# Moving the adaLN product of a two-layer hybrid trunk in among the weight stages, and handing norm sums, mixed blocks and the store over block by block

## The chip, the cores and the metric

The kernel runs on one core of a Trainium2 chip. The metric is the time on the device in microseconds (us), the median of several runs. TensorE is called PE, VectorE DVE, ScalarE ACT, GpSimd POOL and SyncE SP, as in the profile.

## The reference, cut to what matters

Sequence of 512 tokens, model width 1024, float32 throughout, two layers with weights of their own.

```python
c_act = silu(c)                                   # one row of 1024
for l in range(2):
    ada = c_act @ w_ada[l] + b_ada[l]             # 1024 x 6144, a matrix-vector product
    sh1, sc1, g1, sh2, sc2, g2 = split(ada, 6)
    h = rms_norm(x, norm1_g[l]) * (1 + sc1) + sh1
    z, xbc, dt, q, k, v, gate_s, gate_a = split(h @ w_in[l])
    y_ssm = mamba2(z, conv4(xbc), dt) @ w_ssm_out[l]
    y_att = diff_attention(q, k, v) @ w_attn_out[l]
    mixed = sigmoid(gate_s) * y_ssm + sigmoid(gate_a) * y_att
    x = x + g1 * (mixed @ w_out[l])
    h = rms_norm(x, norm2_g[l]) * (1 + sc2) + sh2
    x = x + g2 * (square(relu(h @ w_ff1[l])) @ w_ff2[l])
return rms_norm(x, final_g)
```

Norm 1 needs sh1 and sc1 only; g1 is needed after attention, sh2 and sc2 at norm 2, g2 in the second half of the feed-forward.

## The kernel before

Activations lie transposed, as 8 blocks k of 128 channels by 512 tokens. A weight matrix is streamed as units of 1024 x 256 (1 MB). There are 88 of them in a layer, in this order: 4 for B and C (bc) and 8 for the conv input (xs), together the conv stages; 8 gates; 16 of z and ssm_out; 12 of q, k and v; 4 attn_out (AO); 4 out (WO); 32 of the feed-forward (ff), which run as 4 rounds of 4 units of w_ff1 and 4 of w_ff2. Units alternate between two slots. Three pipelined steps stand ahead of PE's use of a unit:

- SP loads it into `raw[slot]`, once POOL has finished the unit two before (`lo_ready`, L311 and `units`).
- ACT rounds it to `w_hi[slot]` (`convert`, L732). It waits for the load, and for PE to be done with the unit two before (`gemm_done`).
- POOL forms the rest `w_lo[slot]` in four instructions (`low`, L1485).

PE then does 48 matmuls, three products (hi*hi, hi*lo, lo*hi) for each of 8 blocks k and 2 halves j of the unit (`unit_rows`, L384 to L386); k is the outer loop, so both output banks are complete at the end of the unit together. ACT and DVE empty the banks. **Every engine's program is one fixed list**, written out by hand; engines meet only through semaphores. In the lists that matter here, unit n+2 is converted on ACT ahead of the evacuation of unit n:

- Conv stages: ACT converts unit n+2, then seeds the two conv blocks of unit n (L791); DVE adds three taps to each (L1187), ACT takes tanh (L797), DVE makes silu of both (L1197).
- Feed-forward, first half of a round: ACT converts unit n+2, then does relu and square of unit n (L1025, L1027), DVE the low part (L1455, L1458), all of which the second half multiplies (`squared`, at its first unit). Second half: DVE alone adds to x (L1464).

The **adaLN product** has 24 pieces of 1 MB per layer. It stands at the start of each layer, ahead of norm 1 and of all units. Twelve pieces go through DVE: a multiply and seven multiply-adds of 256 columns (L1130, L1134), then PE sums the partitions in 4 instructions (L454). Twelve go through PE (L448), in `raw`, and back through ACT (L772) and 48 small matmuls (L462). Then comes norm 1 (L1090, L749, L1095), block by block, and the product for dt (L471); a long chain of small DVE operations on dt stands ahead of the first taps.

At a norm, ACT squares the 8 blocks of x (L744), DVE sums them (L1071, L1073), PE sums over partitions (L424), DVE takes the mean (L1078), POOL the rsqrt (L1478), PE spreads it (L430). All of this begins when the last block of x is complete. `mixed` is handed from DVE to ACT in the same way after the last block, and `out` is stored by one DMA after the last block of y_out.

The loops over layers, the bc and xs rounds and the ff rounds are hardware loops (`Fori`).

## Time and profile before

| | us |
|---|---|
| median of 3 runs (lowest, highest) | 2994.64 (2994.18, 3003.76) |
| the profiled execution, its own time | 3004.83 |
| its span, first to last instruction | 3003.0 |
| PE / DVE / ACT / POOL busy in the span | 2574.0 / 1322.4 / 960.4 / 1086.1 |
| raw and ada loads | 224 of 1 MB |
| mean granted clock of TensorE | 0.914 |

Times in rows are us from the start of the span. A row of the timeline gives start, length, engine, line, operation, tiles, count, and in brackets how long the engine had been idle and what ended that. Rows of merged instructions (xN) run from the first to the end of the last. Matmuls are pipelined, so that PE's busy time says little; the distance from one to the next, or from one unit to the next, is what to read.

### The profile page before, as it was taken

To read this page: it belongs to the slowest core of one execution; us is meant where nothing else is said; L and a number is where in the kernel's file an instruction comes from. 1 tells how busy PE (TensorE), PEld (TensorE's weight loads), DVE (VectorE), ACT (ScalarE), POOL (GpSimd) and SP (SyncE) were. 2 spreads that over 40 slices of the span, in tenths; PEclk is the share of its full clock that TensorE was granted. 3 is DMA by queue.
4 is the path that set the end of the run, shared out by engine and by line. 5 is a ranking of instruction groups with operands and counts; after the bars stand their busy time and mean duration, and the time that the engine had idled before them with its cause. 6 is when DMAs were issued, how large, how long until landed. Compare 5 with 4: busy or idle time off the path is not lost.

```text
span 3003.0 us, 36626 instructions
## 1 busy us (share of the span) xinstructions
PE 2574.0 (86%) x12200; PEld 2051.4 (68%) x12200; DVE 1322.4 (44%) x2019; ACT 960.4 (32%) x1532; POOL 1086.1 (36%) x825
## 2 busy tenths in 40 slices
PE   5798889788888697999977988988898877799997
PEld 2586667687666476888735866676776655688885
DVE  5654434332655326333366444433335552343333
ACT  1244332322544223222212443332334442232221
POOL 0244343334322144555402443433343222445552
PEclk9899989899989698999978999998999977899998
DMA  7421111122111121222273211011121111212221
GB/s 300 175 84 70 42 42 42 66 75 77 59 55 43 43 91 64 98 98 98 97 302 116 84 57 52 32 57 70 70 91 56 43 43 57 84 71 98 98 98 56
DMA packets 34516, 251.56 MB, mean 84 GB/s; under 512 B 3824, under 2 KB 4208, under 8 KB 4976
## 3 DMA queue, kind: packets, MB, share of 16 engines
q1 hardware_dynamic: 34416, 250.30, 22.8%
q8 instruction: 54, 0.88, 0.1%
q14 instruction: 46, 0.38, 0.0%
HBM read 244.00 MB, written 6.29 MB: 83 GB/s over the span
## 4 chain that ended last, share of the span: by engine, by line
issue 51%; POOL 23%; PE 11%; POOLq 9%; DVE 3%; DMA 2%; ACT 1%; DVEq 0%; PEld 0%; PEldq 0%; ACTq 0%; SPq 0%
POOL w_lo L1485 21%; POOLq L1487 7%; PE gemm L384 3%; PE gemm L385 2%; PE gemm L386 2%; PE aux L448 2%; DMA raw<-stream 2%; POOL y_tok L1526 1%; POOL smalls L1478 1%; DVE conv L1187 1%; POOL xdt L1517 1%; POOLq L1522 1%; PE aux L416 0%; POOLq L1518 0%; DVE pre L1090 0%
## 5 line engine op out<-in xcount | busy, mean ns | idle before, releaser
L1485 POOL TENSOR_TENSOR w_lo<-raw,w_hi 128x512 fp32r<-128x512 f32 x704 | 963.9, 1399 | 1590.0 <-ACT w_hi L732 1588.6
L384 PE MATMUL gemm<-h_hi,w_hi 128*128 128x512 f32 x1536 | 647.3, 421 | 37.9 <-POOLq L1487 10.1
L732 ACT ACTIVATE w_hi<-raw 128x2048 fp32r<-128x2048 f32 x176 | 336.6, 1914 | 939.9 <-PE gemm L386 849.3
L385 PE MATMUL gemm<-h_lo,w_hi 128*128 128x512 f32 x1536 | 614.1, 400 | 0.0
L386 PE MATMUL gemm<-h_hi,w_lo 128*128 128x512 f32 x1536 | 613.3, 399 | 0.0
L384 PEld LDWEIGHTS gemm<-h_hi,w_hi 128*128 128x128 f32 x1536 | 298.5, 194 | 135.5 <-issue 59.9
L384 PE MATMUL gemm<-op_hi,w_hi 128*128 128x512 f32 x896 | 362.4, 404 | 26.6 <-POOLq L1487 23.0
L385 PE MATMUL gemm<-op_lo,w_hi 128*128 128x512 f32 x896 | 359.5, 401 | 0.0
L386 PE MATMUL gemm<-op_hi,w_lo 128*128 128x512 f32 x896 | 358.3, 400 | 0.0
L385 PEld LDWEIGHTS gemm<-h_lo,w_hi 128*128 128x128 f32 x1536 | 298.8, 195 | 69.6 <-issue 12.0
L386 PEld LDWEIGHTS gemm<-h_hi,w_lo 128*128 128x128 f32 x1536 | 297.6, 194 | 65.4
L402 PE MATMUL gemm<-w_hi,h_hi 128*128 128x256 f32 x768 | 233.1, 304 | 1.6 <-issue 1.6
L403 PE MATMUL gemm<-w_hi,h_lo 128*128 128x256 f32 x768 | 227.6, 296 | 0.0
L404 PE MATMUL gemm<-w_lo,h_hi 128*128 128x256 f32 x768 | 227.1, 296 | 0.0
L384 PEld LDWEIGHTS gemm<-op_hi,w_hi 128*128 128x128 f32 x896 | 175.1, 195 | 67.5 <-issue 16.2
L386 PEld LDWEIGHTS gemm<-op_hi,w_lo 128*128 128x128 f32 x896 | 174.9, 195 | 37.9
L385 PEld LDWEIGHTS gemm<-op_lo,w_hi 128*128 128x128 f32 x896 | 175.2, 196 | 36.5
L1455 DVE TENSOR_TENSOR usq<-relu 128x512 f32<-128x512 f32 x64 | 93.0, 1453 | 196.7 <-ACTq L1026 191.4
L402 PEld LDWEIGHTS gemm<-w_hi,h_hi 128*128 128x128 f32 x768 | 158.9, 207 | 10.2 <-issue 9.8
L1187 DVE SCALAR_TENSOR_TENSOR conv<-gemm,cw,conv 128x511 f32<-128x511 f32 x144 | 107.8, 749 | 122.6 <-ACT conv L791 98.0
L403 PEld LDWEIGHTS gemm<-w_hi,h_lo 128*128 128x128 f32 x768 | 159.0, 207 | 0.4
L404 PEld LDWEIGHTS gemm<-w_lo,h_hi 128*128 128x128 f32 x768 | 157.9, 206 | 0.0
(171 smaller groups left out, 2861.3 us busy)
## 6 DMA issues: line engine op xcount, KB each, us to landing
raw<-stream SPq DMA_DIRECT2D x200, 1024.0 KB, 4.8
ada_raw<-stream SPq DMA_DIRECT2D x24, 1024.0 KB, 7.2
xsave<-x SPq DMA_DIRECT2D x2, 2048.0 KB, 12.6
x<-xsave SPq DMA_DIRECT2D x2, 2048.0 KB, 7.8
x<-xT SPq DMA_DIRECT2D x1, 2048.0 KB, 7.7
out<-y_out SPq DMA_DIRECT2D x1, 2048.0 KB, 6.3
dtw_raw<-dtw SPq DMA_DIRECT2D x2, 512.0 KB, 8.0
rope_cos<-ropes SPq DMA_DIRECT2D x2, 256.0 KB, 2.7
```

The lines of the kernel that those rows point to most:

```text
L384: mm(o, w_hi[:, slot, k, cols], hi[:, k, :], start=k == 0, stop=False)
L385: mm(o, w_hi[:, slot, k, cols], lo[:, k, :], start=False, stop=False)
L386: last = mm(o, w_lo[:, slot, k, cols], hi[:, k, :], start=False, stop=k == KB - 1)
L402: mm(o, h_hi[:, k, toks], w_hi[:, slot, k, :], start=k == 0, stop=False)
L403: mm(o, h_lo[:, k, toks], w_hi[:, slot, k, :], start=False, stop=False)
L404: last = mm(o, h_hi[:, k, toks], w_lo[:, slot, k, :], start=False, stop=k == KB - 1)
L448: last = mm(ab[2 + s][0:1, 0:UW], cact[:, k:k + 1], raw[:, s, k, :], start=k == 0, stop=k == KB - 1)
L732: A(w_hi[:, slot], raw[:, slot], ACT.Copy).then_inc(hi_ready, 1)
L1187: last = STT(conv[:, c, lag:S], gb[c][:, 0:S - lag], cw[:, bass.ds(block * CONV + (CONV - 1 - lag), 1)], conv[:, c, lag:S], ALU.mult, ALU.add)
L1455: TT(usq[:, j], relu[:, c], relu[:, c], ALU.mult)
L1485: gp.tensor_tensor(w_lo[:, slot, ks], raw[:, slot, ks], w_hi[:, slot, ks].bitcast(F32), ALU.subtract)
L1487: pool.drain().then_inc(lo_ready, 1)
```

## The change

The adaLN product is spread out. **FIRST**: 8 pieces of layer 0 (sh1, sc1), all loaded at the start into 8 places of their own; 4 go through PE directly, with the piece as the stationary operand (16 float32 matmuls), 4 through DVE. **EARLY**: 12 pieces of layer 0 in its 12 conv units, one behind each unit's silu on DVE. **LATE**: 28 pieces (4 of layer 0, all 24 of layer 1) in the feed-forward of layer 0, one behind each unit's work on DVE. Early and late pieces have two buffers each, and go through DVE only. Their loads are issued by SP between the loads of the units; PE sums each over the partitions behind the next unit. Layer 1 computes nothing of it at its start.

Squares and sums of the norms, `mixed` with its high and low parts, and the store of `out` go block by block. In units whose operands are ready, PE does half j = 0 before j = 1. The bc, xs and ff loops on SP, PE and DVE and the layer loops are written out. x is saved to `xsave` in layer 1 only.

```diff
-ADA_H, ADA_Q, UNITS_H = ADA // 2, ADA // 4, UNITS // 2
+FIRST = [(0, m) for m in (4, 0, 5, 1, 6, 2, 7, 3)]
+EARLY = [(0, m) for m in range(8, 20)]
+LATE = [(0, m) for m in range(20, 24)] + [(1, m) for m in range(ADA)]
+N_FIRST, N_EARLY, N_LATE = len(FIRST) // 2, len(EARLY), len(LATE)
+LATE_ROUND = 8
...
         def sp_program(sp):
+            def unit(l, n):
+                if l * UNITS + n >= 2:
+                    sp.wait_ge(lo_ready, l * UNITS + n - 1 + LO_CREDIT)
+                load(l, n)
...
+            for n in range(N_FIRST):
+                piece(ada_pe[n], *FIRST[2 * n], pe_in[n])
+                piece(ada_first[n], *FIRST[2 * n + 1], first_in[n])
+                if n == 0:
+                    sp.dma_start(x[:], xT).then_inc(x_in, 16)
+                    load_par(0)
+                    load_dtw(0)
+            for l in range(DEPTH):
+                for n in range(U_GATE):
+                    unit(l, n)
+                    if l and n == 1:
+                        sp.wait_ge(S_["layer"], l + LAYER_CREDIT)
+                        sp.dma_start(xsave, x[:]).then_inc(x_saved, 16)
+                    if l == 0:
+                        if n == 0:
+                            sp.wait_ge(ada_step, step_at(N_FIRST - 1))
+                        elif n == 1:
+                            sp.wait_ge(aux_full[2], total_at(l, "start", "bank2", 0) + 1)
+                        else:
+                            sp.wait_ge(ada_step, step_at(N_FIRST + n - 2))
+                        piece(ada_early[n % 2], *EARLY[n], early_in[n % 2])
...
+                for n in range(U_FF, UNITS):
+                    unit(l, n)
+                    i, u = divmod(n - U_FF, 8)
...
+                    m = i * LATE_ROUND + u
+                    if l == 0 and m < N_LATE:
+                        if m == 0:
+                            sp.wait_ge(S_["mixed"], total_at(l, "mix", "mixed", KB))
+                        if m >= 2:
+                            sp.wait_ge(ada_step, step_at(N_FIRST + N_EARLY + m - 2))
+                        piece(ada_late[m % 2], *LATE[m], late_in[m % 2])
...
+            for k in range(KB):
+                sp.wait_ge(S_["pre"], DEPTH * TOTAL["pre"] + k + 1)
+                sp.dma_start(out[:, k], y_out[:, k]).then_inc(out_done, 16)
...
         def pe_program(pe):
+            def ada_piece(where, bank, c):
+                for j in range(2):
+                    for k in range(KB):
+                        last = mm(bank[:, c + j:c + j + 1], where[:, k, j * P:(j + 1) * P], cact[:, k:k + 1], ...)
+            def ada_column(n, acc, bank, c):
+                pe.wait_ge(ada_step, step_at(n))
+                for j in range(2):
+                    last = mm(bank[:, c + j:c + j + 1], acc[:, n % 2, j * P:(j + 1) * P], ones[:, 0:1], start=True, stop=True)
+                last.then_inc(ada_out, 1)
...
+                if l:
+                    norm_spread(st)
+                if l == 0:
+                    for n in range(N_FIRST):
+                        pe.wait_ge(pe_in[n], 16)
+                        ada_piece(ada_pe[n], ab[3], 2 * FIRST[2 * n][1])
+                        ada_column(n, ada_acc, ab[3], 2 * FIRST[2 * n + 1][1])
+                    pe.drain().then_inc(ada_full, 1)
+                    norm_spread(st)
...
+                for i in range(4):
                     sf = Step(l, "ff", i)
                     for u in range(4):
...
+                        if l == 0 and i * LATE_ROUND + u:
+                            late(i * LATE_ROUND + u - 1)
                     for u in range(4):
...
+                        if l == 0 and i * LATE_ROUND + u + 3 < N_LATE:
+                            late(i * LATE_ROUND + u + 3)
...
         def act_program(act):
                 for u in range(N_WO):
-                    convert(l, U_WO // 2 + 1 + u // 2, u % 2)
-                act.wait_ge(S_["x_sum"], st("x_sum") + 1)
-                squares_of_x(st)
+                    if u < N_WO - 1:
+                        convert(l, U_WO // 2 + 1 + u // 2, u % 2)
+                    squares_of_x(st, range(2 * u, 2 * u + 2))
+                convert(l, U_WO // 2 + 1 + (N_WO - 1) // 2, (N_WO - 1) % 2)
...
         def dve_program(dve):
+                def early(n):
+                    if l == 0:
+                        ada_piece(N_FIRST + n, ada_early[n % 2], (early_in[n % 2], (n // 2 + 1) * 16), ada_acc)
                 def conv_round(step, base, block, dst):
                     for c in range(4):
                         taps(step, base, c // 2, c % 2, block + c)
                         if c % 2:
                             silu(step, c - 1, dst(c - 1))
                             silu(step, c, dst(c))
+                            early(2 * base + c // 2)
...
+                for i in range(4):
                     for u in range(4):
                         for j in range(2):
...
+                        late(i * LATE_ROUND + u)
                     for u in range(4):
                         for j in range(2):
...
+                        if i < 3:
+                            late(i * LATE_ROUND + 4 + u)
```

The waits in front of `convert` on ACT, and its place ahead of the seeds and the relus, are the same in both kernels. On POOL the program of the last norm is the same; at norm 2 the rsqrt stands behind `low` of the first two ff units, as before.

## Rows read from the trace of the kernel before

**Rows 1.** Timeline of a ff round, layer 0: ACT, DVE, then POOL.
```profile
1246.20 1.92 ACT L732 ACTIVATE w_hi<-raw 128x2048 fp32r<-128x2048 f32 x1 [8.96 <-PE gemm L386]
...
1248.67 1.37 DVE L1455 TENSOR_TENSOR usq<-relu 128x512 f32<-128x512 f32 x1 [12.59 <-ACTq L1026]
...
1253.51 1.62 DVE L1458 TENSOR_TENSOR op_lo<-usq,op_hi 128x512 fp32r<-128x512 f32 x1
...
1248.20 6.39 POOL L1485 TENSOR_TENSOR w_lo<-raw,w_hi 128x512 fp32r<-128x512 f32 x4 [5.85 <-ACT w_hi L732]
...
1302.60 5.03 POOL L1485 TENSOR_TENSOR w_lo<-raw,w_hi 128x512 fp32r<-128x512 f32 x4 [5.85 <-ACT w_hi L732]
```

**Rows 2.** Timeline of DVE, one adaLN piece; below it, of PE, its sum.
```profile
27.70 0.35 DVE L1130 TENSOR_SCALAR ada_acc<-ada_raw,first 128x256 f32<-128x256 f32 x1 [1.01 <-issue]
...
28.09 3.61 DVE L1134 SCALAR_TENSOR_TENSOR ada_acc<-ada_raw,first,ada_acc 128x256 f32<-128x256 f32 x7
...
35.16 0.61 PE L454 MATMUL aux<-first,ada_acc 128*128 128x1 f32 x4
```

**Rows 3.** DMA issues of the page: count, KB each, median us to landing.
```profile
raw<-stream SPq DMA_DIRECT2D x200, 1024.0 KB, 4.8
ada_raw<-stream SPq DMA_DIRECT2D x24, 1024.0 KB, 7.2
...
out<-y_out SPq DMA_DIRECT2D x1, 2048.0 KB, 6.3
```

**Rows 4.** Timeline of the conv stages, layer 0: ACT, then DVE.
```profile
175.40 1.92 ACT L732 ACTIVATE w_hi<-raw 128x2048 fp32r<-128x2048 f32 x1 [1.75 <-PE gemm L386]
...
256.44 1.92 ACT L732 ACTIVATE w_hi<-raw 128x2048 fp32r<-128x2048 f32 x1 [1.82 <-PE gemm L386]
...
150.97 1.30 DVE L1197 SCALAR_TENSOR_TENSOR bct<-ctanh,conv 128x512 f32 x2 [0.25 <-issue]
...
183.92 1.30 DVE L1197 SCALAR_TENSOR_TENSOR bct<-ctanh,conv 128x512 f32 x2 [0.25 <-issue]
```

**Rows 5.** Timeline, start of layer 0: first squares, the sum over partitions, norm 1.
```profile
16.69 1.13 ACT L744 ACTIVATE sq<-x 128x512 f32<-128x512 f32 x2
...
24.62 1.86 PE L424 MATMUL aux<-first,ss 128*128 128x1 f32 x8 [24.62 <-DVEq L1076]
...
103.67 1.41 DVE L1090 SCALAR_TENSOR_TENSOR pre<-x,amul,aux 128x512 f32<-128x512 f32 x2 [0.18 <-issue]
```

**Rows 6.** Timeline of DVE, end of layer 0 to the first taps of layer 1.
```profile
1495.77 1.43 DVE L1464 SCALAR_TENSOR_TENSOR x<-gemm,ada,x 128x512 f32<-128x512 f32 x2 [9.45 <-PE gemm L386]
...
1591.16 1.41 DVE L1090 SCALAR_TENSOR_TENSOR pre<-x,amul,aux 128x512 f32<-128x512 f32 x2 [0.18 <-issue]
...
1632.24 0.75 DVE L1187 SCALAR_TENSOR_TENSOR conv<-gemm,cw,conv 128x511 f32<-128x511 f32 x1 [0.53 <-issue]
```

**Rows 7.** Timeline, end of attn_out to the first ff unit, layer 0: ACT, DVE.
```profile
1077.50 1.91 ACT L732 ACTIVATE w_hi<-raw 128x2048 fp32r<-128x2048 f32 x1 [8.96 <-PE gemm L386]
...
1094.26 1.92 ACT L732 ACTIVATE w_hi<-raw 128x2048 fp32r<-128x2048 f32 x1 [9.97 <-PE gemm L386]
...
1159.16 1.92 ACT L732 ACTIVATE w_hi<-raw 128x2048 fp32r<-128x2048 f32 x1 [3.51 <-PE gemm L386]
...
1126.23 1.43 DVE L1443 SCALAR_TENSOR_TENSOR x<-gemm,first,x 128x512 f32<-128x512 f32 x2 [9.45 <-PE gemm L386]
...
1144.24 1.41 DVE L1090 SCALAR_TENSOR_TENSOR pre<-x,amul,aux 128x512 f32<-128x512 f32 x2 [3.37 <-PE aux L430]
```

**Rows 8.** Timeline of DVE, the last norm.
```profile
2977.14 1.43 DVE L1464 SCALAR_TENSOR_TENSOR x<-gemm,ada,x 128x512 f32<-128x512 f32 x2 [9.45 <-PE gemm L386]
...
2980.05 5.39 DVE L1073 TENSOR_TENSOR ss<-ss,sq 128x512 f32<-128x512 f32 x7
...
2990.96 5.36 DVE L1090 SCALAR_TENSOR_TENSOR y_out<-x,con,aux 128x512 f32<-128x512 f32 x8 [3.30 <-PE aux L430]
```

**Rows 9.** The page's granted clock of TensorE in 40 slices, tenths of full speed.
```profile
PEclk9899989899989698999978999998999977899998
```

More of the change, by code:

```diff
@@ L1064, in dve_program, with norm_add @@
             dve.drain().then_inc(ready, 1)
-            def norm_sums(step):
-                for k in range(KB):
+            def norm_add(step, ks):
+                for k in ks:
                     dve.wait_ge(S_["sq"], step("sq") + 1)
@@ L1079, in norm_sums, with ada_piece, take_ada, scales @@
                 dve.drain().then_inc(S_["ms"], 1)
+            def ada_piece(n, where, landed, acc):
+                dve.wait_ge(*landed)
+                for k in range(KB):
+                    if k == 0:
+                        dve.wait_ge(ada_out, n - 1 + OUT_CREDIT)
+                        TS(acc[:, n % 2], where[:, 0], cact[:, 0:1], None, ALU.mult).then_inc(ada_step, 1)
+                    else:
+                        dve.wait_ge(ada_step, n * KB + k)
+                        STT(acc[:, n % 2], where[:, k], cact[:, k:k + 1], acc[:, n % 2], ALU.mult, ALU.add)\
+                            .then_inc(ada_step, 1)
+            def take_ada(nth, l, bank, c, first, last):
+                dve.wait_ge(ada_full, nth)
+                cols = slice(first * KB, last * KB)
+                dve.wait_ge(par_in, (l + 1) * 16)
+                TT(ada[:, cols], bank[:, c:c + (last - first) * KB],
+                   par[:, C_BADA + first * KB:C_BADA + last * KB], ALU.add)
+                dve.drain().then_inc(ada_read, 1)
+            def scales(m):
+                scale_at, norm_at = ((1, C_N1), (4, C_N2))[m]
+                STT(amul[:, m * KB:(m + 1) * KB], ada_v[:, scale_at, :], 1.0,
+                    par[:, norm_at:norm_at + KB], ALU.add, ALU.mult)
+                settle()
             def norm(step, mul, shift):
@@ L1489, in pool_program @@
             pool.sem_inc(lo_ready, LO_CREDIT)
-            pool.sem_inc(ada_out, 2)
             pool.wait_ge(ready, 1)
-            with pool.Fori(0, DEPTH) as l:
+            for l in range(DEPTH):
                 st = Step(l, "start")
+                if l:
+                    low(l, 0, 0)
                 rsqrt(ms, rs, st, "ms", "rs")
-                low(l, 0, 0)
+                if l == 0:
+                    low(l, 0, 0)
                 low(l, 0, 1)
```

380 lines of the change are left out of this document (214 added, 166 removed).

## The prediction

> **What bounds the kernel now.** I read the timeline first, one stage at a time, because the page calls PE 86% busy and that hides which stages run at PE's own pace. In a feed-forward round [rows 1] POOL starts the low part of one unit at 1248.20 and that of the fifth after it at 1302.60: 10.88 us per unit, with nothing between units. That is PE's pace at full clock, and ACT, DVE and POOL have slack: ACT starts converting unit n+2 when unit n is done (1246.20, I call this moment C), POOL is done with it at C + 8.4 (C + 7.2 where it takes 5.03), and PE wants it at C + 10.9. The conv stages run close to this (C from 175.40 to 256.44, [rows 4]). What stands outside that pace is the start of a layer: the adaLN product keeps norm 1 waiting until 103.67 in layer 0 [rows 5], and from 1496.4, where the last unit ends, to 1591.16 in layer 1 [rows 6]. Then come norm 2, the step from attn_out to out, and the tail.
>
> So the change removes real path. The question is what 40 pieces cost where they go, and the timeline of those stages holds the answer too: the order inside [rows 1] is convert of n+2 first, then relu, squares and low part of unit n, ended on DVE at 1255.13 (1253.51 + 1.62), which is C + 8.9. In the conv stages it is convert of n+2, then seeds, taps, tanh and silu of unit n, ended at C + 9.8 (175.40 to 185.22, [rows 4]).
>
> **What the change gains.**
>
> *Norm 1, layer 0.* x now lands behind two pieces, with 4.4 MB queued up to it in place of the 2.3 MB, and ACT squares it first. In the old order squares begin at 16.69 behind the parameters and dt's weights, and the sums end at 24.6 [rows 5]; I put them at about 21.5. The first piece began 3.1 behind the sums (27.70, [rows 2]); dt's low part and the parameter work now come in between, some 2 more; then four pieces of 4.0 (0.35 + 3.61 and one start): 42.6. PE does its 4 pieces, 16 matmuls each, which are 32 instructions (its 2 column sums are 4 in [rows 2]). At the 0.15 us of its column sums (0.61 for 4, [rows 2]) one takes 4.9, at the 0.23 of the cold sums (1.86 for 8, [rows 5]) 7.4. With a column sum behind each that ends at 23.5 + 22 = 45.5, or 55.5. Norm 1 then begins at 45.5 to 58. PE warms up while it works, so I take 46: a gain of 58 us (46 to 60).
>
> *Layer 1's start.* After the last unit at 1496.4: one add to x (0.75, half of 1495.77's row), square and sum of the last block (1.7, from half of 1.13 in [rows 5] and a seventh of 5.39 in [rows 8], with two hand-overs), the take of the last sixth of ada (0.5), then mean, rsqrt and spread, 5.5 us by the last norm (sums end 2985.44, y_out begins 2990.96, [rows 8]). Norm 1 begins 8.9 after the end of the unit, at 1505.3 in place of 1591.16. Behind it stands dt's chain up to the first taps at 1632.24, unchanged but for a convert of 1.9 on ACT that now stands ahead of norm 1: 86 + 1, so **87 us** (85 to 90).
>
> *Out units.* From convert to convert 1077.50 to 1094.26 is 16.8 [rows 7] where PE's pace gives 10.9. With 2 blocks left to hand over instead of 8 PE starts at once; ACT's convert then comes a little behind the last two: 5 us per layer, 10 (8 to 12).
>
> *Norm 2.* Squares, sums and mean end 9.8 us earlier, but POOL's rsqrt stands behind the low part of the second ff unit, whose convert ACT now does after the last squares: convert from D + 1.5, low part until D + 8.7 (5.03 and waits), rsqrt 1.0, spread 2.1, with D the end of the out units, 1126.1. Norm 2 begins at D + 12.1, not at D + 18.1 (1144.24, [rows 7]): 6 us per layer, 12 (10 to 20).
>
> *The tail.* Sums end at D + 2.5 in place of 2985.44 with D = 2977.1 [rows 8], 5.9 earlier; the store of 2 MB takes 6.3 to land [rows 3], the last eighth perhaps 2.7: 9.5 (6 to 10).
>
> Gains: 58 + 87 + 10 + 12 + 9.5 = **177 us**. Half order j by itself I cost at nothing: convert stands ahead of every evacuation and waits for both halves. So do the written-out loops: at the round boundaries inside the rows above PE's pace has no gap. Between -5 and +10.
>
> **What it costs.** SP's list now reads: load unit n; wait for piece n-2; load piece n; load unit n+1. Piece n-2 stands on DVE behind the silu (or the low part) of unit n-2, and these stand on ACT behind the convert of unit n. **That is a loop**: convert n, evacuation of n-2, piece n-2, loads of piece n and unit n+1, convert n+1. Before, the load of n+1 waited for POOL alone, with a unit's time to spare. `raw` has two places, but the wait in SP's list takes the second away.
>
> Its length: 9.8 + 4.0 (piece) + 0.2 + landing. A load alone lands in 4.8, one with others in flight in 7.2 [rows 3]. The unit's load goes 0.3 behind the piece, through the same engines: I take 7.2 from the piece's issue, with 5.1 and 8.5 as the ends. In the conv stages 21.2 per unit, in the first half of an ff round 8.9 + 4.0 + 0.2 + 7.2 = 20.3, against 10.9.
>
> *Conv stages, layer 0.* In the old times: silu of unit 0 ends at 152.3 (150.97 + 1.30, [rows 4]), piece 0 at 156.3, unit 3 lands at 163.7; nine turns of 21.2 bring the convert of unit 12 to 354.5, where it was 256.44. The tail adds little: piece 10 at 368, taps and silu of unit 11 (7), piece 11 (4), sum and take (1) end at 380.6; before, about 279.5 (convert of unit 13 at 268, 9.8, and 1.5 of transposes). **+101 us**. The PE column sums (12 of 0.6, [rows 2]) vanish in PE's idle time.
>
> *Feed-forward, layer 0.* Count from the convert C that starts when unit 0 of a round is done. Four turns bring the convert of unit 6 to C + 81.2. From there PE is the bound: unit 6 may start at + 8.4, and it, 7 and 8 take 10.9 + 2 x 11.4 (with a column sum each) up to + 42.1. In the second half a piece follows the adds to x directly, so its loads (issued 5.2 after the unit's end, landed 12.6) are in time. A round takes 123.3 in place of 87.0: 3 x 36.3 = 109. In the last round pieces stop after the fourth: one turn (20.3), then 78 to its end, 98.4 for 76.2: 22. Together 131.
>
> Here a row speaks for more. In the second half a piece (two operands in SBUF) runs beside POOL's low part. In [rows 1] POOL's four instructions take 6.39 beside DVE's squares, 5.03 alone, and DVE's own take 1.37 to 1.62 there. Pieces of 6.5 instead of 4.0, and 8 for POOL, push the second halves past PE's pace by about 2.5 us each and more at the change of halves: +10 (0 to 20). The Trainium skill (SBUF — State Buffer, on the port pair that VectorE and GpSimd share) says that a VectorE instruction with two SBUF inputs and a GpSimd one that reads SBUF exclude each other for their whole length. By that the pieces would be nearer the upper end, +16. The rows agree that both get slower. Feed-forward: **+141 us**.
>
> **The sum.** 101 + 141 - 177 = **+65 us**. It is made against the profiled execution (3004.83, of which 3003.0 is span), which lies 10.2 above the median of the runs shown. I carry the difference over to the median: 2994.6 + 65 = **3060 us**, 2.2% slower. The turns of the two loops enter some 23 times, so 1 us in a turn is 23 us in the result.
>
> **Rivals.**
>
> *The pieces ride free.* DVE is 44% busy, the DMA engines mostly idle, and if each load were in raw by the time its convert can start, only the column sums (about 20 us) and 6 us at the end of the conv stages would be left: 177 - 26 gained, **2844**. It takes a turn of no more than 10.9 + the 2.5 to 3.7 of slack that ACT and POOL leave. Against it: the landing alone is 4.8, the evacuation 8.9. It decides only if the order convert, evacuation, piece, load is not what binds, for example if pieces were done by DVE before the evacuation. 0.12.
>
> *The clock falls.* PE would now idle some 9 us in every 20 in the bound halves. The granted clock falls with gaps in PE's work: it is 6 tenths from 975 to 1050, where attention runs out, 7 and 8 from 1500 to 1650, around the adaLN product of layer 1, and 9 in the dense stages [rows 9]; of its two levels, 1.2 and 2.4 GHz, that is the lower for part of the time. In a turn a unit at half speed (twice 10.9) still fits, as PE is not the bound there; but at each change to the second half and at the conv stages' end a slow unit adds up to 10: 3 x 10 + 10, **3100**. The Trainium skill (TensorE: Matmul & The Clock Gate, on oscillation of the gate) warns of just such a rhythm of work and waits. 0.10.
>
> *Lighter loops.* The second load lands close to the first's time, 5.1, and PE's pieces are quick: 2.1 x 23 = 48 less, **3012**, or about no change with every gain at its upper end. 0.08.
>
> *The first part does not help.* The eight pieces ahead of norm 1 are as late as the old product because eleven MB stand in one queue. But the second of two loads lands 2.4 behind the first (7.2 less 4.8, [rows 3]), so eleven are in by about 31, ahead of the last piece: unlikely; +20 at worst, **3080**, inside the range.
>
> **How the numbers follow.** Forecast 0.67, free pieces 0.12, clock 0.10, lighter loops 0.08, rest 0.03. The range of **3000 to 3110** takes in the cases of the clock and of the lighter loops, and the bounds of the landing (-48, +30) and of the port (-10, +10) laid on the forecast; it leaves out the free pieces alone. What a measurement can tell from no change is about 0.3%, 9 us: faster 0.13, same 0.04, slower 0.83.
>
> **What would show it.** In the profile after: on layer 0's conv stages converts 21 us apart, with SP's wait for DVE's pieces (not POOL) ahead of each load, and ACT's convert waiting for the DMA; in layer 0's feed-forward four slow units and four at PE's pace; layer 1's same stages at their old pace; norm 1 of layer 0 near 46, that of layer 1 some 9 us behind the last unit, norm 2 12 us behind; POOL's rsqrt there behind its low part. I am wrong if layer 0's converts stay 11 to 12 us apart, or if the wait before them is for PE.

## The result and the profile after

The changed kernel takes **3052.17 us** (median of 4 runs, 3052.11 to 3055.09), the kernel before 2994.85 in the same comparison: a ratio of 1.0187, 95% interval 1.0167 to 1.0207. The profiled execution took 3052.11 us, 3050.3 of it span. The forecast was 3060 with a range of 3000 to 3110, slower with 0.83.

First the page, the lines that answer to [rows 3, 9] and the convert's own line:

```profile
span 3050.3 us, 33323 instructions
...
PE 2541.0 (83%) x11928; PEld 2068.2 (68%) x11928; DVE 1440.2 (47%) x2182; ACT 949.4 (31%) x1508; POOL 1101.7 (36%) x825
...
PEclk9888899998999698889898999989989996999999
...
L820 ACT ACTIVATE w_hi<-raw 128x2048 fp32r<-128x2048 f32 x176 | 336.7, 1914 | 1134.1 <-DMA raw<-stream 448.1
...
raw<-stream SPq DMA_DIRECT2D x176, 1024.0 KB, 4.8
```

Read the convert's line (L820), ACT's rounding of a unit: of its 1134 us of idle time 448 now end with the arrival of a load (35 waits) and 685 with PE. In the kernel before it was one wait of 9 us for a load and 929 us for PE. Yet half of the loads still land in 4.8 us or less. The transfers aren't slow, they are issued late. Why is in the waits of SP's queue:

```profile
engine line waited for: us in total, times, longest us
SPq L327 <- POOLq L1651: 2049.0, 133, 45.0
SPq L323 <- DVE late_acc L1200: 427.3, 26, 42.3
SPq L323 <- DVE ada_acc L1200: 240.1, 11, 32.2
```

Of the 176 loads of units only 133 still wait for POOL. 37 pieces wait for DVE, 667 us in all, and unit loads stand behind them. One turn in the conv stages, unit by unit the answer to [rows 4] (ACT, DVE, then SP):

```profile
196.13 1.92 ACT L820 ACTIVATE w_hi<-raw 128x2048 fp32r<-128x2048 f32 x1 [12.05 <-DMA raw<-stream]
...
216.41 1.92 ACT L820 ACTIVATE w_hi<-raw 128x2048 fp32r<-128x2048 f32 x1 [10.08 <-DMA raw<-stream]
...
203.82 1.29 DVE L1325 SCALAR_TENSOR_TENSOR xsf<-ctanh,conv 128x512 f32<-128x512 f32 x2
...
205.41 3.61 DVE L1200 SCALAR_TENSOR_TENSOR ada_acc<-ada_early,first,ada_acc 128x256 f32<-128x256 f32 x7
...
209.05 0.33 SPq L323 DMA_DIRECT2D ada_early<-stream  x1
209.42 0.43 SPq L327 DMA_DIRECT2D raw<-stream  x1
```

The convert starts at 196.13, the silus end 9.0 later, the piece 3.9 after that, SP issues at once (209.05, and the unit's load at 209.42), and the next convert starts at 216.41: a turn of 20.3 us. The same in the feed-forward, where a piece of the second half looks different (DVE, then POOL; compare [rows 1, 2]):

```profile
1205.90 3.61 DVE L1200 SCALAR_TENSOR_TENSOR late_acc<-ada_late,first,late_acc 128x256 f32<-128x256 f32 x7
...
1267.75 7.33 DVE L1200 SCALAR_TENSOR_TENSOR late_acc<-ada_late,first,late_acc 128x256 f32<-128x256 f32 x7
...
1268.69 5.58 POOL L1649 TENSOR_TENSOR w_lo<-raw,w_hi 128x512 fp32r<-128x512 f32 x4 [2.68 <-ACT w_hi L820]
```

And the norms (timeline: PE's first piece and its column sum, DVE at norm 1 of layer 0, at norm 2, at layer 1's start, at the end; they answer to [rows 5 to 8]):

```profile
22.19 6.97 PE L458 MATMUL aux<-first,ada_pe 128*128 128x1 f32 x32
29.01 0.99 PE L466 MATMUL aux<-first,ada_acc 128*128 128x1 f32 x4
...
53.13 0.17 DVE L1208 TENSOR_TENSOR ada<-aux,par 128x16 f32<-128x16 f32 x1 [11.33 <-PEq L518]
...
55.39 1.41 DVE L1228 SCALAR_TENSOR_TENSOR pre<-x,amul,aux 128x512 f32<-128x512 f32 x2 [1.79 <-PE aux L504]
...
1149.22 0.75 DVE L1581 SCALAR_TENSOR_TENSOR x<-gemm,g1h,x 128x512 f32<-128x512 f32 x1 [4.43 <-PE gemm L441]
...
1160.82 1.40 DVE L1228 SCALAR_TENSOR_TENSOR pre<-x,amul,aux 128x512 f32<-128x512 f32 x2 [7.83 <-PE aux L504]
...
1666.28 0.75 DVE L1620 SCALAR_TENSOR_TENSOR x<-gemm,ada,x 128x512 f32<-128x512 f32 x1 [1.52 <-PE gemm L441]
...
1673.84 1.41 DVE L1228 SCALAR_TENSOR_TENSOR pre<-x,amul,aux 128x512 f32<-128x512 f32 x2 [3.30 <-PE aux L504]
...
3042.28 5.36 DVE L1228 SCALAR_TENSOR_TENSOR y_out<-x,con,aux 128x512 f32<-128x512 f32 x8 [3.27 <-PE aux L504]
```

To see where the time went I laid the starts of ACT's converts side by side (176 in each trace, 88 per layer). Each figure is the length of a stretch in us:

| stretch, from convert to convert | before, layer 0 / 1 | after, layer 0 / 1 |
|---|---|---|
| start to unit 2 (layer 1: from unit 87 of layer 0) | 134.9 / 148.1 | 86.7 / 54.6 |
| conv stages, 2 to 12 | 121.6 / 121.5 | 211.2 / 123.8 |
| 12 to 20 (end of conv, scan) | 213.1 / 206.4 | 208.7 / 206.1 |
| 20 to 50 (z, attention) | 575.4 / 575.6 | 566.5 / 565.7 |
| 50 to 58 (attn_out, out, norm 2) | 114.3 / 114.3 | 102.8 / 103.1 |
| feed-forward, 58 to 87 | 315.5 / 315.5 | 468.7 / 315.6 |
| unit 87 of layer 1 to the end | 46.9 | 36.9 |

Two stretches lose (the ones in which layer 0 carries pieces: 90 and 153 us), layer 1's same stretches stay. And one line nobody had on the bill: z and attention are 8.8 and 9.9 us shorter, though no edit touches them.

### The profile page after: what moved, and what is told of

It reads as the page before. It is cut to its first block, busy times and chain, and to the rows that moved or that the text cites. A ratio compares the mean times of both kernels' runs of the same rounds, so it can differ in the third digit from the quotient of the medians.

```text
span 3050.3 us, 33323 instructions
## 1 busy us (share of the span) xinstructions
PE 2541.0 (83%) x11928; PEld 2068.2 (68%) x11928; DVE 1440.2 (47%) x2182; ACT 949.4 (31%) x1508; POOL 1101.7 (36%) x825
## 4 chain that ended last, share of the span: by engine, by line
issue 39%; POOL 19%; PE 14%; DVE 10%; POOLq 7%; ACT 4%; DMA 3%; DVEq 2%; ACTq 1%; SPq 0%; PEldq 0%; PEld 0%
POOL w_lo L1649 17%; POOLq L1651 6%; DMA raw<-stream 2%; DVE conv L1315 2%; PE gemm L428 2%; PE gemm L430 2%; PE gemm L429 2%; DVE ada_acc L1200 1%; PE gemm L439 1%; PE gemm L441 1%; PE gemm L440 1%; ACT probs L1052 1%; PE aux L458 1%; PE aux L488 1%; POOL y_tok L1694 1%
## 5 line engine op out<-in xcount | busy, mean ns | idle before, releaser
L1649 POOL TENSOR_TENSOR w_lo<-raw,w_hi 128x512 fp32r<-128x512 f32 x704 | 978.1, 1419 | 1673.3 <-ACT w_hi L820 1672.2
L820 ACT ACTIVATE w_hi<-raw 128x2048 fp32r<-128x2048 f32 x176 | 336.7, 1914 | 1134.1 <-DMA raw<-stream 448.1
L439 PE MATMUL gemm<-h_hi,w_hi 128*128 128x512 f32 x960 | 394.7, 411 | 12.0 <-DVE conv L1315 7.0
L440 PE MATMUL gemm<-h_lo,w_hi 128*128 128x512 f32 x960 | 388.8, 405 | 0.0
L441 PE MATMUL gemm<-h_hi,w_lo 128*128 128x512 f32 x960 | 387.4, 404 | 0.0
L428 PE MATMUL gemm<-h_hi,w_hi 128*128 128x512 f32 x576 | 263.6, 458 | 10.2 <-DVE h_lo L1233 4.9
L430 PE MATMUL gemm<-h_hi,w_lo 128*128 128x512 f32 x576 | 234.0, 406 | 0.0
L429 PE MATMUL gemm<-h_lo,w_hi 128*128 128x512 f32 x576 | 233.7, 406 | 0.0
L439 PEld LDWEIGHTS gemm<-h_hi,w_hi 128*128 128x128 f32 x960 | 191.2, 199 | 53.0 <-issue 7.4
L441 PEld LDWEIGHTS gemm<-h_hi,w_lo 128*128 128x128 f32 x960 | 189.5, 197 | 42.0
L440 PEld LDWEIGHTS gemm<-h_lo,w_hi 128*128 128x128 f32 x960 | 190.5, 198 | 39.7
L1601 DVE TENSOR_TENSOR usq<-relu 128x512 f32<-128x512 f32 x64 | 93.5, 1462 | 244.9 <-ACTq L1133 241.9
L440 PE MATMUL gemm<-op_lo,w_hi 128*128 128x512 f32 x512 | 203.0, 396 | 0.0
L441 PE MATMUL gemm<-op_hi,w_lo 128*128 128x512 f32 x512 | 203.0, 396 | 0.0
```

The lines of the kernel that those rows point to most:

```text
L428: mm(o, w_hi[:, slot, k, cols], hi[:, k, :], start=k == 0, stop=False)
L429: mm(o, w_hi[:, slot, k, cols], lo[:, k, :], start=False, stop=False)
L430: last = mm(o, w_lo[:, slot, k, cols], hi[:, k, :], start=False, stop=k == KB - 1)
L439: mm(o, w_hi[:, slot, k, cols], hi[:, k, :], start=k == 0, stop=False)
L440: mm(o, w_hi[:, slot, k, cols], lo[:, k, :], start=False, stop=False)
L441: last = mm(o, w_lo[:, slot, k, cols], hi[:, k, :], start=False, stop=k == KB - 1)
```

## Experiments

All ratios are against the kernel before, run on the same chip in the same comparison (median 2998.92 us for conv_order, both_order, both_lag and warm, 3001.25 for before_written_out, rows_order, rsqrt_first and warm18, 2999.88 for piece_first, split, all_three and all_split).

| kernel | us | ratio, 95% interval |
|---|---|---|
| conv_order | 2983.23 | 0.9959 (0.9938 to 0.9979) |
| both_order | 2866.05 | 0.9557 (0.9534 to 0.9579) |
| both_lag | 2840.14 | 0.9474 (0.9457 to 0.9492) |
| piece_first | 2836.81 | 0.9466 (0.9429 to 0.9503) |
| warm | 3053.27 | 1.0184 (1.0165 to 1.0204) |
| warm18 | 3057.64 | 1.0182 (1.0165 to 1.0199) |
| before_written_out | 2978.95 | 0.9926 (0.9912 to 0.9940) |
| rows_order | 3058.97 | 1.0185 (1.0169 to 1.0201) |
| rsqrt_first | 2830.74 | 0.9434 (0.9421 to 0.9447) |
| split | 2831.77 | 0.9439 (0.9423 to 0.9455) |
| all_three | 2866.10 | 0.9550 (0.9534 to 0.9565) |
| all_split | 2870.36 | 0.9568 (0.9553 to 0.9583) |

### The loop, cut at SP

`upto(l, n)` issues the loads of units, each with its wait for POOL as before, up to unit n.

```diff
 for n in range(U_GATE):
-    unit(l, n)
+    upto(l, n + 2)          # conv_order, both_order
     ...
     piece(ada_early[n % 2], *EARLY[n], early_in[n % 2])
 for n in range(U_FF, UNITS):
-    unit(l, n)
+    upto(l, n + 2)          # both_order alone
```

> The changed kernel with one edit in SP's list: in layer 0's conv stages the load of unit n+2 is issued ahead of the wait for piece n-2 and the load of piece n (it was unit n ahead of them). Same loads, same work on DVE, nothing moved in the feed-forward. Theory 1 (the loop convert n, evacuation of n-2, piece n-2 on DVE, SP's wait, load of n+1): the wait no longer stands ahead of a load that is wanted soon, so the turn of 20.3 us is gone. What is left is PE: the column sum of piece n-1 stands ahead of unit n+1 and waits for DVE, which is done with piece n-1 at 13 us behind the end of unit n-1; then 0.6 and 10.9 us: 24.5 per two units, 12.3 each. Ten turns give back 8.0 each: 3052 - 80 = 2972 us, converts 12 to 13 us apart, ACT's wait there for PE and not for the DMA. Rival 2 (DVE's 4 us per piece, or two streams of loads side by side, are what costs, in whatever order): converts stay about 20 us apart and the time stays at 3045 to 3055. Rival 3 (landing slows with two loads in flight, part of the cost): converts 14 to 17 us apart, 2990 to 3015 us.

> As conv_order, and the same order (unit n+2 ahead of piece n) in layer 0's feed-forward. Theory 1: in the first half of a round units go at 12.3 us by the same column sum (0.6 behind a DVE that is done 13 us after the unit's end) and in the second half at 11.5, plus some 10 us over the stage for pieces beside POOL's low part; the stage's loss against the kernel before falls from 153 us to 35 (16 x 1.4 + 12 x 0.6 + 5 to 10): 2972 - 118 = 2855 us, 4.7% faster than the kernel before. Rival 2 (work or bandwidth): no change in the feed-forward, about the time of conv_order. Rival 3 (DVE and POOL on the same memory port cost most of the feed-forward's 153 us): gives back under half, 2900 to 2930 us.

conv_order: 2983 us, 69 below the changed kernel's median (73.9 by the spans, 2976.4 against 3050.3) where 80 was expected; converts 12.3 apart from unit 8 on, ACT waiting for PE. both_order: 2866 where 2855 was expected. SP's queue in both_order:

```profile
SPq L327 <- POOLq L1658: 2452.3, 171, 62.1
...
SPq L323 <- DVE ada_acc L1207: 67.9, 10, 14.6
SPq L323 <- DVE late_acc L1207: 66.6, 25, 4.3
```

The pieces' waits for DVE fall from 667 to 135 us, and the unit loads wait for POOL again (171 times). The same transfers, the same work on DVE, 186 us less: **the order of SP's list was the cost.** DVE's work as such, or two streams of loads side by side, could not have given it back. The first conv units did not come down to 12.3, though: at unit 1's end PE had waited 12.63 us for piece 0, which on DVE stands behind dt's chain and the first taps, to add up its column (timeline of PE in conv_order):

```profile
110.97 0.99 PE L473 MATMUL aux<-first,ada_acc 128*128 128x1 f32 x4 [12.63 <-DVE ada_acc L1207]
```

That is why conv_order's stretch from unit 2 to unit 12 is 138.0 us and not the 131 that were expected; by the spans it is the whole of its miss (6 us). both_order misses by 11 by its median and by 16 by its span: 5 of these lie in the same stretch, 7 in the feed-forward (below), and the rest of layer 0 adds 3 (6 more up to the scan's end, 3 less in z and attention).

both_lag also moves PE's column sum of a piece one unit back:

```diff
 for slot in range(2):
     unit(l, i + U_BC // 2, slot, h_hi, h_lo)
-    if i or slot:
-        early(2 * i + slot - 1)
+    early(2 * i + slot - 2)
```

and so on in the other stages (in the feed-forward columns 2 and 3 both behind unit 4, since DVE takes them there).

> As both_order, and PE adds up the column of a piece one unit later (behind unit n the column of piece n-2, not n-1), in the conv stages and the feed-forward. Theory 1 with PE's wait for DVE as the bound that comes next: DVE is done with piece n-2 long before, so units go at 10.9 + 0.6 = 11.5 us in both stages; against both_order 0.8 us less for each of 11 conv units and 16 feed-forward units, about 20 us: 2835 us. If PE's wait at the column sums is not what binds in both_order (but ACT's and DVE's own chain of 11 to 12 us, or the pieces beside POOL), the time stays within 5 us of both_order.

2840 us, 26 less than both_order. The gain lies in the feed-forward: its stretch falls from 357 to 331 us, with 11.4 from convert to convert, that is PE's 10.9 and 0.5 of column sum. In both_order two converts in most rounds came 15.0 after the one before: PE's column stood waiting for a piece of the first half (1.79 us at 1242.32), as expected. That wait is half of the 3.6 us. The other half lies behind it: the matmuls from 1243.69 to 1246.67 come 0.43 us apart instead of 0.23, with a granted clock of 0.83 over 1240 to 1250 and 1.00 in the 10 us on either side. In the conv stages the edit gave 0.4 us in all up to unit 12. From unit 8 on the converts are 12.2 apart, where the kernel before has 11.8, so that the column sum (0.5) shows there too. Ahead of unit 8 PE no longer waits for piece 0, but five pieces now take 7.2 to 7.3 us on DVE, where conv_order and both_order had one such; the next section shows what these are.

### The loop, cut at DVE

```diff
 def conv_round(step, base, block, dst):
     for c in range(4):
+        if c % 2 == 0:
+            early(2 * base + c // 2)
         taps(step, base, c // 2, c % 2, block + c)
         if c % 2:
             silu(step, c - 1, dst(c - 1))
             silu(step, c, dst(c))
-            early(2 * base + c // 2)
```

The same in the other conv rounds, and ahead of the squares in the first half of a feed-forward round.

> The changed kernel with SP's list and PE's order untouched; only on DVE each piece goes ahead of the taps of its conv unit, and in the first half of a feed-forward round ahead of the squares (it was behind them). A second test of the loop, from its other side: if it is the order convert, evacuation, piece, loads that binds, then piece n-2 no longer stands behind the evacuation of n-2 but behind that of n-3: the convert of n+1 comes 8.9 + 4.0 + 7.4 = 20.3 us behind that of n-1, not of n, which is 10.2 us per unit and so hidden below PE's 10.9 + 0.6. And the piece runs before POOL's low part of the next unit begins, so it keeps its 3.61 us instead of 7.25. Theory: conv units 12.2 us apart (the pace of the kernel before), the stretch from unit 2 to unit 12 back from 211 to 122 to 125 us, the feed-forward of layer 0 from 469 to 331 to 336: 3052 - 87 - 135 = 2830 us (2825 to 2850). Rival (loads or DVE's work as such, or SP's position alone is what matters): converts stay 20 us apart, 3052 us.

2837 us, where 2830 was expected (the conv stages take 128 and the feed-forward 342, for 122 to 125 and 331 to 336). SP's list is that of the changed kernel, and its waits for the pieces are still 462 us, but they end in time. The loop can be cut at either of its two orders, which is what makes it a loop and not a slow step. The feed-forward stretch is 342 us, 11 over both_lag, since in the second halves neither order was changed. Timeline of DVE and of POOL in the conv stages, first of rsqrt_first (below; there DVE has the old order), then of piece_first:

```profile
102.73 7.25 DVE L1210 SCALAR_TENSOR_TENSOR ada_acc<-ada_early,first,ada_acc 128x256 f32<-128x256 f32 x7
109.89 4.93 DVE L1325 SCALAR_TENSOR_TENSOR conv<-gemm,cw,conv 128x511 f32<-128x511 f32 x6
114.96 1.29 DVE L1335 SCALAR_TENSOR_TENSOR bct<-ctanh,conv 128x512 f32<-128x512 f32 x2
...
116.56 7.25 DVE L1210 SCALAR_TENSOR_TENSOR ada_acc<-ada_early,first,ada_acc 128x256 f32<-128x256 f32 x7
```

```profile
163.41 3.61 DVE L1200 SCALAR_TENSOR_TENSOR ada_acc<-ada_early,first,ada_acc 128x256 f32<-128x256 f32 x7
...
168.61 5.05 POOL L1650 TENSOR_TENSOR w_lo<-raw,w_hi 128x512 fp32r<-128x512 f32 x4 [7.45 <-ACT w_hi L820]
```

In the first DVE has no gap between the units: 13.8 us per unit, all its own work, 7.25 of it a piece beside POOL's low part. In the second the piece is over before the low part begins (168.61) and takes 3.61, and from unit 3 on the units go at 11.4 to 12.5. That is what took the place of PE's wait for piece 0.

### Norm 1 of layer 0: why PE's pieces took 6.97 us

```diff
+for _ in range(10):          # warm; 18 in warm18
+    mm(ab[1][0:2, 0:NCON], ones[:, 0:2], con[:, 0:NCON], start=True, stop=True)
 for l in range(DEPTH):
```

> The changed kernel with 10 matmuls of 408 columns (con against two columns of ones, result unused) on PE ahead of the column sums of norm 1 in layer 0, so that PE works from about 8 us on. It tells why PE's four pieces took 6.97 us each and not 4.9. Theory A (they ran at the lower of PE's two clock levels all through 22 to 53 us, and work ahead of them brings the higher): the instructions take 0.15 us in place of 0.214, a piece 4.9, norm 1 of layer 0 begins at 46 to 48 in place of 55.4, and the time falls by 8 to 9 us to 3043. Theory B (a product of 128 columns of weights with one column takes 0.214 us whatever the clock, since it hangs on the load of the weights): the pieces stay at 6.97 us and the time at 3052, or 1 or 2 us over it.

> As warm, with 18 wide matmuls instead of 10, so that they last until the column sums of norm 1 at about 20 us. With 10 they went from 0.72 to 0.36 us apart at 9.0 us (the higher clock level), ended at 14.1, PE was idle for 6.1 us, and the pieces ran at granted clock 0.50, 6.96 us each. Theory A (the pieces' 0.214 us per product is the lower clock level): the pieces now begin at the higher one; the first of them take 3.5 to 5 us, and norm 1 begins earlier by as much as the clock lasts (all four: at 46 us, time 3043). A variant of A: products of one column don't keep the clock up, so that it falls in the first or second piece and norm 1 gains 2 to 4 us only. Theory B (0.214 us whatever the clock): the pieces stay at 6.96 us each while the granted clock is 1.0, and the time at 3052.

Timeline of PE in warm (among it its weight loads, PEld, whose distance is that of the wide matmuls' instructions; these have 432 columns, not the 408 of the expectation, and each matmul is two instructions), then in warm18:

```profile
9.23 0.09 PEld L508 LDWEIGHTS aux<-con,first 128*2 128x2 f32 x1 [0.59 <-issue]
9.60 0.09 PEld L508 LDWEIGHTS aux<-con,first 128*2 128x2 f32 x1 [0.28 <-issue]
...
4.24 9.87 PE L508 MATMUL aux<-con,first 128*2 128x432 f32 x20 [4.24 <-DVEq L1172]
20.24 1.86 PE L496 MATMUL aux<-first,ss 128*128 128x1 f32 x8 [6.12 <-DVEq L1186]
21.96 6.96 PE L458 MATMUL aux<-first,ada_pe 128*128 128x1 f32 x32
```

```profile
4.20 15.76 PE L508 MATMUL aux<-con,first 128*2 128x432 f32 x36 [4.20 <-DVEq L1172]
20.76 1.05 PE L496 MATMUL aux<-first,ss 128*128 128x1 f32 x8 [0.80 <-DVEq L1186]
21.68 5.75 PE L458 MATMUL aux<-first,ada_pe 128*128 128x1 f32 x32
...
28.97 6.96 PE L458 MATMUL aux<-first,ada_pe 128*128 128x1 f32 x32
```

Both whole times stayed where they were (3053 and 3058, ratios 1.0184 and 1.0182 to the 1.0187 of the changed kernel). But the rows of warm18 tell the cause: straight behind the wide matmuls eight sums over partitions take 1.05 us (1.86 in warm, behind 6.1 us of idling), the first piece 5.75, and from the second on it is 6.96 again, though PE never paused for more than 0.7 us. The granted clock in that run is 0.65 from 20 to 30 us and 0.50, the lower level, from 30 to 54. So theory B falls (the first products are quicker while the clock is higher), and so does plain A. The variant is what the rows show, though norm 1 begins only 0.9 us earlier (54.49, not 55.39) and not 2 to 4: **in these runs a row of products of one column neither kept TensorE at its higher clock level nor brought it there**, in 33 us without a pause (warm, 20.24 to 53.08, granted clock 0.50). For the changed kernel itself the profile gives a clock of 1.00 over 20 to 56 us, but its pieces take 6.97 us as warm's take 6.96; that it was the lower level there is read from warm.

### The two terms priced at nothing

```diff
-with pe.Fori(0, DEPTH) as l:
+for l in range(DEPTH):
```

on all five engines of the kernel before; and, in the changed kernel, `unit` with its old order of rows in place of `unit_column`.

> The kernel before with one edit: the loop over the two layers is written out on all five engines (a loop over a register in it), so that the layer's number is a constant in every wait and address. Nothing else of the change. My prediction priced this at nothing; the trace of the changed kernel shows attention, which no edit touches, 6 us shorter in each layer and the z stage 2.5. Theory: that is this edit; the waits of an engine no longer need an addition on registers, 0.1 to 0.3 us at each hand-over on a chain. Then attention is 5 to 6 us shorter per layer here too, z 2, and the whole time falls by 15 to 25 us (the other stages' chains gain a little as well): 2970 to 2980 us. Rival: it stems from elsewhere (the order of a unit's halves, the state that other stages leave), then attention stays at 298.7 us between the converts of units 38 and 50, and the time within 3 us of 2995.

> The changed kernel with a unit's matmuls in the old order (both halves row by row, not half 0 and then half 1). Priced at nothing in the prediction. It should tell whether the evacuation of 8.9 us in the bound conv stages (9.8 in the kernel before) comes from half 0 being ready early. If it does, each of the 21 or so turns of the two loops is up to 0.9 us longer: 3052 + 10 to 19 us. If the 0.9 comes from the written-out loops, the time stays within 4 us of 3052, since ACT converts unit n+2 ahead of the evacuation and that waits for both halves anyway.

rows_order gives 1.0185, the changed kernel 1.0187: the order of the halves is worth nothing that these runs can tell, and its evacuation takes 9.0 us too. Writing out the layers is worth 0.74% (0.60 to 0.88), 22 us, with nothing else of the change. It is attention (298.8 to 291.9 us between the converts of units 38 and 50 of layer 0, 298.6 to 292.5 in layer 1), z (2.8 and 1.2) and the stretch with the scan (7.0 and 3.1). The first sums of squares show it in small, DVE in the kernel before and with the layers written out:

```profile
19.40 0.69 DVE L1073 TENSOR_TENSOR ss<-ss,sq 128x512 f32<-128x512 f32 x1 [0.16 <-issue]
```

```profile
19.32 5.39 DVE L1073 TENSOR_TENSOR ss<-ss,sq 128x512 f32<-128x512 f32 x7
```

0.16 us of "issue" ahead of each of seven dependent instructions is gone. All that the edit changed at this line is the number in the wait. The taps of before_written_out confirm it within one run: in the bc units and the later xs units, which still stand in hardware loops, gaps of 0.16 to 0.18 us stay ahead of them and the evacuation takes 9.8 us or more; in the first xs unit, which stands in none, they are gone and it takes 9.0. That answers what rows_order asked: the shorter evacuation comes from the written-out loops. Where a chain passes through many such hand-overs it adds up; where PE is the bound (feed-forward, 315.5 in both) it is worth nothing.

### Towards a better version

rsqrt_first is both_lag with one line of POOL moved:

```diff
-low(l, U_FF // 2, 0); low(l, U_FF // 2, 1)
-rsqrt(ms, rs, st, "ms", "rs")
+low(l, U_FF // 2, 0)
+rsqrt(ms, rs, st, "ms", "rs")
+low(l, U_FF // 2, 1)
```

> As both_lag, and at norm 2 POOL does rsqrt ahead of the low part of the second feed-forward unit instead of behind it. In the changed kernel that low part began at 1152.56, 0.3 us ahead of the mean (1152.83), and rsqrt at 1157.65. Theory: rsqrt at 1152.9, norm 2 begins 4.7 us earlier in both layers, and the low part, then done at about 1159, is still there before PE has finished the first feed-forward unit: 9 us less than both_lag, 2831 us. Rival: the first feed-forward unit is held by something else (ACT's convert or h_lo), then within 3 us of both_lag.

2830.74, where 2831 was expected, and rsqrt stands ahead (timeline of POOL, the changed kernel, then rsqrt_first):

```profile
1152.56 4.92 POOL L1649 TENSOR_TENSOR w_lo<-raw,w_hi 128x512 fp32r<-128x512 f32 x4 [6.23 <-ACT w_hi L820]
1157.65 1.01 POOL L1642 TENSOR_TENSOR smalls<-smalls 128x4 f32<-128x4 f32 x1 [0.18 <-issue]
```

```profile
1073.90 1.01 POOL L1652 TENSOR_TENSOR smalls<-smalls 128x4 f32<-128x4 f32 x1 [6.78 <-DVEq L1197]
```

split gives DVE five of the first eight pieces and PE three:

```diff
+FIRST_PE = [FIRST[0], FIRST[2], FIRST[4]]
+FIRST_DVE = [FIRST[1], FIRST[3], FIRST[5], FIRST[7], FIRST[6]]
...
```

> As rsqrt_first, and of the eight pieces ahead of norm 1 of layer 0 DVE takes five and PE three (it was four and four). In the changed kernel PE's four take 6.97 + 0.99 us each at the lower clock level and end at 53 us, while DVE is done at about 42 and waits 11.3 us. Theory: PE's three end 7.7 us earlier, with two more column sums of 0.7 behind DVE's fifth piece (42 to 46 us): norm 1 begins at 49 to 50 us in place of 55.4, and the time falls by 5 to 6 us against rsqrt_first, to 2825. Rival (the fifth piece waits for its load, or dt's part on the way is what bounds): less than 2 us.

The time is 2832, not 2825. Norm 1 did begin at 49.78, and the convert of unit 12 came 4.9 us earlier (215.9, not 220.8), but unit 14's came at 273.0 and 273.1. The 4.9 us were lost between the last conv unit and the scan. PE idles there while the last pieces are done, and its clock was back later. Granted clock (the last three figures of a row are PEclk, DMA share, GB/s) in rsqrt_first, then in split:

```profile
240.00:250.00 10.00, 5.89 (x22) 5.28 (x22) 5.94 (x14) 4.04 (x8) 2.25 (x3) 0.50 0.31 107
250.00:260.00 10.00, 9.71 (x52) 7.53 (x51) 2.94 (x5) 3.21 (x6) 9.33 (x9) 0.96 0.00 0
```

```profile
240.00:250.00 10.00, 7.41 (x26) 6.23 (x27) 1.79 (x6) 1.37 (x4) 6.54 (x7) 0.50 0.01 2
250.00:260.00 10.00, 10.00 (x36) 7.48 (x36) 2.90 (x5) 3.01 (x5) 4.59 (x5) 0.69 0.00 1
```

From 250 to 260 split runs at 0.69 on average where the other has 0.96: 36 matmuls where the other does 52 in 9.71 us. A miss for the whole, though the step worked. What makes the clock rise sooner in the one than in the other is open, and so is whether split has to do with it: the stretch from unit 12 to unit 20 takes 205.7 to 222.6 us in layer 0 of the fourteen traces, and in layer 1, where the edits of these experiments change next to nothing, 203.0 to 216.2.

> As rsqrt_first (SP's units two ahead, PE's columns one unit later, rsqrt first), and on DVE each piece ahead of its unit's taps or squares as in piece_first. In rsqrt_first units 2 to 8 of the conv stages are 13.8 us apart, with DVE busy without a gap: taps 4.93, silu 1.29, piece 0.35 + 7.25, the last beside POOL's low part; from unit 8 on the piece takes 3.61 and the units 12.3. Theory (the phase between DVE's piece and POOL's low part sets the piece's length, and that sets the pace): pieces of 3.61 from the start, units at 12.2, 9 to 12 us less: 2820 us. Rival (phase falls in with POOL anyway): within 3 us of 2831.

> As all_three, with the eight first pieces split five and three as in split. If the two gains add: 2831 - 10 - 6 = 2815 us, 6% faster than the kernel before. If pieces ahead of the taps take away what split gives (both act on the start of layer 0), 2820.

Both are misses, by 46 and 50 to 55 us: instead of gaining on rsqrt_first they lose 35 and 40. Timeline of DVE, then of POOL, in all_three:

```profile
193.67 0.35 DVE L1206 TENSOR_SCALAR ada_acc<-ada_early,first 128x256 f32<-128x256 f32 x1 [1.40 <-PE aux L473]
194.06 7.24 DVE L1210 SCALAR_TENSOR_TENSOR ada_acc<-ada_early,first,ada_acc 128x256 f32<-128x256 f32 x7
201.22 4.92 DVE L1325 SCALAR_TENSOR_TENSOR conv<-gemm,cw,conv 128x511 f32<-128x511 f32 x6
...
194.32 5.66 POOL L1660 TENSOR_TENSOR w_lo<-raw,w_hi 128x512 fp32r<-128x512 f32 x4 [8.67 <-ACT w_hi L830]
```

With PE's column of piece n-2 put behind unit n, `ada_acc` (two places) is free for piece n only when unit n is done, so the piece that was to go ahead of the taps waits for PE (1.40 us) and starts together with POOL's low part. It takes 7.24 us, the taps come after it, and a unit takes 15.4. Each of the two edits is good, and the one takes away what the other needs. That accounts for 17 of the 38 us between the spans (units 2 to 12: 151.6 us, not 134.4). Another 16 lie between units 12 and 20, and there the rows only show that the clock was lower (0.69 over the 49 us between the converts of units 13 and 14, against 0.83 over 40 us): why is not shown. SP's order with the pieces ahead of the taps but without the later columns wasn't tried; an estimate from piece_first's rows is that its conv stages would go at 11.4 to 12.2. The best measured is rsqrt_first, 5.7% faster than the kernel before and 7.4% than the changed one (0.9434 by 1.0187).

## Why the prediction was right, and where it wasn't

The sum was +65; between the two profiled executions it is 47.3 (3050.3 less 3003.0), between the medians 57.3. The profiled execution of the kernel before lay 10 above its median, which the prediction said and carried over; that of the changed kernel lay on its median. So against the traces, from which its terms were read, the sum is 17.7 too high, against the medians only 7.7, and that difference is luck. Point by point, from the table of stretches:

- **The loop** is as described, and the three orders at SP and the one on DVE show it. Its turn was put at 21.2 us (9.8 + 4.0 + 0.2 + 7.2) in the conv stages; it measured 20.1 to 20.5, since the evacuation takes 9.0. Conv stages: forecast 101, measured 89.6 up to unit 12 and 5.5 more up to 14, 95.
- **Feed-forward**: forecast 141, measured 153. Turns of 20.3 to 21.9 in place of 20.3 in the first halves, and the two slow pieces of 6.3 to 8.2 us in each second half. Both were in the sum, the second with 10 (0 to 20), so the rest of 12 lies within its bounds.
- **Norm 1 of layer 0**: forecast a start at 46, measured 55.39; the stretch gains 48.2, not 58. The step that failed is "PE warms up while it works, so I take 46". Of the two prices the prediction gave for an instruction of a piece (0.15 and 0.23 us), 0.214 is what it took (6.97 / 32 from start to start), for the reason that warm18 shows. The end I had kept for the range, 55.5, was the right one.
- **Layer 1's start**: forecast 87. Norm 1 begins 7.6 behind the last add to x (forecast 8.9 behind the unit), the stretch gains 93.5, and the conv stages behind it give 2.3 back: 91.
- **Out units, norm 2, tail**: forecast 10, 12 and 9.5, measured 11.8 (49.4 to 43.5 twice), 10.9 and 10.1. POOL's rsqrt stood behind the low part as foretold, norm 2 begins 11.6 behind the last add to x, and rsqrt_first shows the price of that place: against both_lag 7.7 us in two layers by the stretches from unit 54 to unit 58, 9.4 by the medians and 12 by the ratios, which come from two comparisons.
- **The written-out loops at nothing**: wrong, and the largest error. The argument was that at the round boundaries of the feed-forward PE has no gap. That holds for loops over rounds in PE-bound stages. It missed that the register of the layer loop enters nearly every wait in the kernel, in attention and z too, where chains of short instructions are the bound. The bound of -5 was too tight; it is -22 (before_written_out). In the two traces the stretches that no piece and no handover touches are 29 us shorter together; the 10 us by which the trace of the kernel before lies above its median may be part of that.
- **Half order at nothing**: right.
- **The clock rival** (3100): the granted clock did fall in the bound halves, 0.88 over 1176 to 1660 us, 0.83 over 115 to 300, against 1.00 and 0.95 in the kernel before. The stages came out within 12 us of their terms without it, so it cost little, as PE was mostly not the bound there; what it cost at the changes of halves no row separates. The Trainium skill (TensorE: Matmul & The Clock Gate, on oscillation of the gate) warned of this rhythm, and the trace agrees as to the clock, not as to a price.
- **The port rule.** The piece beside POOL's low part takes 7.24 to 7.33 us against 3.61 alone, POOL's part 5.66 against 5.05. In all_three's rows the piece is alone for 0.26 us before and 1.3 after POOL, so it did some 2.0 of its 3.6 us of work in POOL's 5.66. The Trainium skill (SBUF — State Buffer, on the shared port pair) says that the two exclude each other. An estimate by that, from the two lengths alone, is 8.7 us for both together, and they take 7.2 to 7.3; the trace agrees that they hold each other up, but not that they exclude each other fully, and nearly all of the delay falls on DVE. The prediction's 6.5 was too low for DVE and its 8 for POOL too high.

So the forecast was near by its mechanism, but nearer than its terms deserve: norm 1 (10 us) and the feed-forward (12) were missed one way, the written-out layers (22) and the conv turns (6) the other.

## What to carry to other kernels

A queue that issues in program order makes every wait in its list a wait of all that stands behind it. Before putting a new transfer with its own condition into such a list, write down the cycle from the load to the work and back to the wait, and put the loads that the bound engine needs ahead of the condition; here that moved 186 us with no transfer and no work added or taken away. A second edit that is good alone has to be checked against the slack that the first one used up, as all_three shows. And a loop register in every semaphore wait is not free where a chain of short instructions is the bound.

## What the runs showed of the hardware that was not expected

- With products of 128 x 128 weights with one column TensorE stayed at its lower clock level in warm: 33 us without a pause at 0.214 us each, granted clock 0.50. In warm18 a clock that was high fell in the first of them (0.65 over 20 to 30 us, 0.50 after). Wide matmuls of 432 columns in the same place in warm came 0.72 us apart up to 9.23, 5 us after their start, and then 0.36.
- A wait of 1.79 us of PE in both_order cost twice its length: for 3 us behind it the matmuls came 0.43 us apart and not 0.23 (granted clock 0.83 over these 10 us).
- DVE's pieces, with both operands in SBUF, took twice as long beside GpSimd's low part (3.61 to 7.3 us), GpSimd's part 12% longer (5.05 to 5.66). In both_lag and rsqrt_first the units go at 13.5 to 13.8 us while the two meet; there it ends by itself, and from unit 8 on the units go at 12.2.
- A register in the waits cost 0.16 us of issue at each of a chain of dependent instructions on DVE; with constants these gaps were gone.
